# Order of the six matmuls of a weight block: by pass over both column halves, or by column half over the three passes

## The chip, the cores and the metric

One core of a Trainium2 chip runs the whole program in one launch. The metric is the device time of one execution in microseconds (us); of several runs the median is taken.

## The reference

One inference step of a two-layer decoder trunk, for a prompt of 512 tokens and 8 sample tokens that share the weights. Everything is float32.

```
x += 0.5 * SwiGLU_a(RMSNorm(x))
x += Mixer(RMSNorm(x))      # layer 0: retention and SSD heads; layer 1: latent attention
x += 0.5 * SwiGLU_b(RMSNorm(x))
...
def swiglu(h, w_in, w_out):
    gate, up = jnp.split(h @ w_in, 2, axis=-1)
    return (jax.nn.silu(gate) * up) @ w_out
```

The model width is 1024, the hidden width of the four FFNs 2816. Most of the work is these dense products: h @ w_in and the product with w_out of the FFNs, and the input and output projections of the two mixers.

## The kernel before

The 520 tokens lie along the free axis, features on the 128 partitions. A dense product is made of weight blocks of 128x128. Float32 accuracy comes from two parts of each operand in float32r: weights as `w_high` (WH) + `w_low` (WL), activations as `x_high` (XH) + `x_low` (XL), or `hidden_high` (HH) + `hidden_low` (HL) in the second product of an FFN. A block is multiplied three times ("passes"): high weights with high activations, high weights with low activations, low weights with high activations. The 520 columns are cut into two halves of 260, and each half of an output tile has an accumulator bank of its own in PSUM. So a block is six matmuls of 260 columns, each with its own weight load.

Weights come in chunks of four blocks (256 KB), issued by SP into four slots (`w_raw`). ScalarE makes the high part (line 330), VectorE the low part (line 336), and TensorE waits for the low part once per chunk (semaphore w_split). The function `gemm` (line 358 is its matmul) goes through the blocks of a step: k (128 rows of the contraction) outside, m (one or two output tiles) inside, so up to four banks are in use; the other four belong to the next step. One semaphore tells when the last matmul of a step is done (acc_full), and only then are the banks read; another tells when a chunk's weights were used (w_used). TensorE's order is written out by hand; the FFN's first product runs in a hardware loop of two steps of 16 blocks, ten times round.

Two places in the latent attention do not use `gemm`. `wo_first` (line 2443) makes the first step of the output projection, the 16 blocks of `("wo", 0)`, and it goes through all blocks for half 0 and then through all of them again for half 1:

```
for half in range(2):
    ...
    for k in range(KD):
        ...
        for m in range(2):
            ...
            for w, x, start, stop in ((wh, XH, ...), (wh, XL, ...), (wl, XH, ...)):
                mm = nc.tensor.matmul(PS[:, b0 + 2 * m + half, 0:TH], w, x[:, k, cols], ...)
```

The steps ("wo", 1) to ("wo", 3) that follow use `gemm` with the same operands XH, XL, WH and WL. The step ("uv", g) (line 2341) makes three passes of 512 columns into one bank, then three into the next.

Of the kernel before, what the change touches and what calls it, by code (L numbers as in the profile page):

```python
# [200 lines left out]
def program(nc, io, phases=PHASES):  # L201
# [66 lines left out]
    def bank0(step):  # L268
        return 4 * plan.set_of[step]
# [19 lines left out]
    def acquire(pe, step, i=None):  # L289

        n = plan.turn_of[step]
        if n:
            pe.wait_ge(acc_free[plan.set_of[step]], n if i is None else n + i)
# [45 lines left out]
    def gemm(pe, step, mtiles, ktiles, rhs, i=None, split=0, before_k=None, cols=TH):  # L339


        acquire(pe, step, i)
        first, b0 = plan.first[step], bank0(step)
        blocks = [(k, m) for k in range(ktiles) for m in range(mtiles)]
        for c in range((len(blocks) + 3) // 4):
            n = first + c
            slot = n % R
            for j, (k, m) in enumerate(blocks[4 * c:4 * c + 4]):
                if before_k and m == 0:
                    before_k(k)  # L350
                if j == 0:
                    pe.wait_ge(w_split, n + 1 if i is None else split * i + (n + 1))
                wh, wl = (w[:, slot, j * P:(j + 1) * P] for w in (WH, WL))
                xh, xl = rhs(k)
                for w, x, start, stop in ((wh, xh, k == 0, False), (wh, xl, False, False),
                                          (wl, xh, False, k == ktiles - 1)):
                    for half in range(2):
                        mm = nc.tensor.matmul(PS[:, b0 + 2 * m + half, 0:cols], w,  # L358
                                              x[:, half * cols:(half + 1) * cols], start=start, stop=stop)
            if 4 * c + 4 >= len(blocks):  # L360
                mm.then_inc(acc_full[plan.set_of[step]], 1)
            else:
                mm.then_inc(w_used, 1)
# [47 lines left out]
    e.XH, e.XH_OFF, e.XL, e.acc, e.acc_free = XH, XH_OFF, XL, acc, acc_free  # L411
    e.acc_full, e.acquire, e.at, e.bank0, e.first_wait = acc_full, acquire, at, bank0, first_wait
    e.gemm, e.halves, e.io, e.nc, e.nn_of = gemm, halves, io, nc, nn_of
    e.out_stored, e.pe_stats, e.phases, e.plan, e.sem = out_stored, pe_stats, phases, plan, sem
    e.w_split, e.w_used, e.wait_free, e.wait_full, e.x_rhs = w_split, w_used, wait_free, wait_full, x_rhs
# [50 lines left out]
    def _(pe):  # L466
        def ffn(f):
            nn = nn_of[f]
            gemm(pe, (f, "in", 0), 2, KD, x_rhs, before_k=first_wait(pe, nn))
            pe_stats(pe, (f, "in", 0), nn)  # L470
            gemm(pe, (f, "in", 1), 2, KD, x_rhs, before_k=spread_at(pe, 3, (f, "in", 0), nn))
            with pe.Fori(0, (KF - 2) // 2) as i:
                for g in (2, 3):
                    gemm(pe, (f, "in", g), 2, KD, x_rhs, i, 8)
            done = KF * (ffn_index[f] + 1)
            h_rhs = lambda k: (HH[:, k, :], HL[:, k, :])
            for g in (0, 1):

                gemm(pe, (f, "out", g), 2, KF, h_rhs,
                     before_k=(lambda k: pe.wait_ge(hl_done, done - KF + k + 1)) if g == 0 else None)  # L480
            for g in (2, 3):
                gemm(pe, (f, "out", g), 2, KF, h_rhs)
# [2429 lines left out]
```

## Time and profile before

| | |
|---|---|
| runs | 2303.39, 2304.45, 2306.28 us; median 2304.45 us |
| span of the profiled execution, first to last instruction | 2300.2 us |
| left around the span, against the median of the runs | 4.25 us |
| TensorE busy, weight loads busy | 98%, 95% of the span |
| VectorE, ScalarE, GpSimd busy | 49%, 35%, 7% |
| mean granted TensorE clock | 0.995 of full speed |

No time of its own is given for the profiled execution, so it is put at its span and the 4.25 us around it, which is the median. Busy times are sums over one engine. A matmul's row lasts longer than its share of the engine, since matmuls overlap; how fast they follow each other is read from their start times. The chain of waits names, for each moment, the instruction that the end of the program hung on.

### The profile page before, as it was taken

The page shows a single profiled execution, that of the slowest core. Times are in us where ns is not written, and L with a number is a line of the kernel's source. Part 1 is how long each engine was busy: PE and PEld are TensorE (multiplying, and loading weights), DVE is VectorE, ACT ScalarE, POOL GpSimd, SP SyncE. Part 2 cuts the span into 40 slices and gives each one's busy share as a digit, 9 for nine tenths or more (in the row PEclk, how much of TensorE's full clock was granted, in tenths as well). Part 3 has the DMA queues.
Part 4 walks back from the last instruction along what each step waited for, and adds up shares of the span by engine and source line. Part 5 has one row for each costly group of instructions (what it writes and reads, how often), then busy time and mean ns, then how long its engine had stood idle before and what let it go on. Part 6 is the DMA issues. An engine that isn't in the chain of part 4 may idle for free.

```text
span 2300.2 us, 48657 instructions
## 1 busy us (share of the span) xinstructions
PE 2258.0 (98%) x19482; PEld 2179.2 (95%) x19482; DVE 1117.0 (49%) x1773; ACT 812.2 (35%) x1420; POOL 170.9 (7%) x243
## 2 busy tenths in 40 slices
PE   9999999999999999999999999999999989999998
PEld 9999999998888999999999999999996689999997
DVE  4444434787436544444334444433557745444433
ACT  4333333462324333333233333233346634333222
POOL 0000001022100010000010000001114411000000
PEclk9999999999999999999999999999999999999999
DMA  4323333233333232333332333333546733323333
GB/s 146 91 91 91 96 101 113 79 98 101 119 118 111 84 100 84 94 92 91 102 102 88 93 92 91 99 102 91 162 151 229 264 99 92 91 91 91 96 102 106
DMA packets 119872, 249.49 MB, mean 108 GB/s; under 512 B 15360, under 2 KB 15632, under 8 KB 118400
## 3 DMA queue, kind: packets, MB, share of 16 engines
q1 hardware_dynamic: 105552, 193.05, 28.1%
q0 software_dynamic: 14048, 54.49, 6.9%
q8 instruction: 99, 1.62, 0.3%
q14 instruction: 29, 0.24, 0.0%
q10 hardware_dynamic: 144, 0.09, 0.0%
HBM read 237.30 MB, written 9.95 MB: 107 GB/s over the span
## 4 chain that ended last, share of the span: by engine, by line
PE 91%; DVE 6%; ACT 2%; issue 1%; DMA 0%; SPq 0%; DVEq 0%; ACTq 0%
PE psum L358 83%; PE psum L2356 1%; PE psum L2371 1%; DVE w_low L336 1%; PE psum L1163 1%; DVE conv_sum L1593 1%; PE psum L2443 1%; DVE probs_by_key L2783 0%; PE psum L2341 0%; PE psum L2401 0%; PE psum L1150 0%; ACT probs L2516 0%; PE psum L2323 0%; PE psum L1008 0%; PE psum L2297 0%
## 5 line engine op out<-in xcount | busy, mean ns | idle before, releaser
L336 DVE TENSOR_TENSOR w_low<-w_raw,w_high 128x512 fp32r<-128x512 f32 x718 | 510.4, 729 | 631.5 <-ACT w_high L330 630.7
L358 PE MATMUL psum<-x_high,w_high 128*128 128x260 f32 x3840 | 773.6, 283 | 5.9 <-DVE w_low L336 2.8
L358 PE MATMUL psum<-x_low,w_high 128*128 128x260 f32 x3840 | 770.5, 282 | 0.0
L358 PE MATMUL psum<-x_high,w_low 128*128 128x260 f32 x3840 | 769.3, 282 | 0.0
L358 PEld LDWEIGHTS psum<-x_high,w_high 128*128 128x128 f32 x3840 | 589.2, 188 | 12.3 <-DVE x_low L640 1.9
L330 ACT ACTIVATE w_high<-w_raw 128x512 fp32r<-128x512 f32 x718 | 433.9, 623 | 463.4 <-PE psum L358 451.6
L358 PEld LDWEIGHTS psum<-x_low,w_high 128*128 128x128 f32 x3840 | 591.8, 189 | 0.0
L358 PEld LDWEIGHTS psum<-x_high,w_low 128*128 128x128 f32 x3840 | 591.0, 188 | 0.0
L358 PE MATMUL psum<-hidden_high,w_low 128*128 128x260 f32 x1408 | 284.0, 283 | 0.0
L358 PE MATMUL psum<-hidden_high,w_high 128*128 128x260 f32 x1408 | 282.9, 282 | 0.0
L358 PE MATMUL psum<-hidden_low,w_high 128*128 128x260 f32 x1408 | 282.9, 282 | 0.0
L663 DVE TENSOR_TENSOR gate_up<-psum,rstd 128x520 f32<-128x520 f32 x176 | 114.9, 695 | 320.7 <-PE psum L358 306.4
L546 ACT ACTIVATE silu_gate<-gate_up 128x520 f32<-128x520 f32 x88 | 56.2, 639 | 528.8 <-DVE gate_up L663 528.5
L358 PEld LDWEIGHTS psum<-hidden_high,w_high 128*128 128x128 f32 x1408 | 217.4, 188 | 0.0
L358 PEld LDWEIGHTS psum<-hidden_high,w_low 128*128 128x128 f32 x1408 | 216.8, 188 | 0.0
L358 PEld LDWEIGHTS psum<-hidden_low,w_high 128*128 128x128 f32 x1408 | 216.7, 188 | 0.0
L553 ACT ACTIVATE hidden_high<-hidden 128x520 f32 (+1 forms) x88 | 56.3, 640 | 126.6 <-DVE hidden L670 126.6
L776 POOL TENSOR_TENSOR square_sums<-squares 128x520 f32<-128x520 f32 x6 | 7.9, 1320 | 1234.9 <-ACT squares L525 1234.9
L2836 POOL DMA_DIRECT2D cache_pages<-in_cache_pages_dram x128 | 68.7, 537 | 129.7 <-issue 124.7
L681 DVE TENSOR_TENSOR hidden_low<-hidden,hidden_high 128x520 f32 (+1 forms) x88 | 61.1, 694 | 3.1 <-ACT hidden_high L553 3.1
L670 DVE TENSOR_TENSOR hidden<-silu_gate,gate_up 128x520 f32<-128x520 f32 x88 | 61.1, 695 | 2.8 <-ACT silu_gate L546 2.8
L525 ACT ACTIVATE squares<-residual 128x1040 f32<-128x1040 f32 x23 | 24.7, 1075 | 91.6 <-DVE residual L695 91.6
(395 smaller groups left out, 1652.5 us busy)
## 6 DMA issues: line engine op xcount, KB each, us to landing
w_raw<-in_weights_dram SPq DMA_DIRECT2D x720, 256.0 KB, 2.7
cache_pages<-in_cache_pages_dram POOLq DMA_DIRECT2D x128, 272.0 KB, 4.3
ret_sample_state<-in_state_ret_dram POOLq DMA_DIRECT2D x2, 2048.0 KB, 8.5
out_ret_s_dram<-ret_sample_state POOLq DMA_DIRECT2D x2, 2048.0 KB, 6.6
out_y_dram<-residual SPq DMA_DIRECT2D x8, 260.0 KB, 2.2
ssm_sample_state<-in_state_ssm_dram POOLq DMA_DIRECT2D x2, 1024.0 KB, 5.6
out_ssm_s_dram<-ssm_sample_state POOLq DMA_DIRECT2D x2, 1024.0 KB, 4.7
residual<-in_x_dram SPq DMA_DIRECT2D x3, 520.0 KB, 6.7
```

Of the source, the lines that this page charges most:

```text
L330: nc.scalar.activation(WH[:, slot, :], WRAW[:, slot, :], ACT.Copy).then_inc(w_high, 1)
L336: nc.vector.tensor_tensor(WL[:, slot, :], WRAW[:, slot, :], WH[:, slot, :].bitcast(F32), ALU.subtract).then_inc(w_split, 1)
L358: mm = nc.tensor.matmul(PS[:, b0 + 2 * m + half, 0:cols], w, x[:, half * cols:(half + 1) * cols], start=start, stop=stop)
L525: nc.scalar.activation(SQT[:], XT[:, 2 * pair:2 * pair + 2, :], ACT.Square).then_inc(squares_done, 1)
L546: nc.scalar.activation(SGT[:, g % 2, :], GU[:, g % 2, 0, :], ACT.Silu).then_inc(silu_done, 1)
L553: nc.scalar.activation(out, src, ACT.Copy).then_inc(hh_done, 1)
L663: ins = nc.vector.tensor_tensor(out[:, 2 * m:2 * m + 2, :], acc(step)[:, 2 * m:2 * m + 2, :], halves(RSTD[:]), ALU.mult)
L670: nc.vector.tensor_tensor(HT[:, g % 2, :], SGT[:, g % 2, :], GU[:, g % 2, 1, :], ALU.mult).then_inc(hid_done, 1)
L681: nc.vector.tensor_tensor(out, src, hi.bitcast(F32), ALU.subtract).then_inc(hl_done, 1)
L1163: nc.tensor.matmul(PS[:, b + m, jt * P:NP_], VTOK[:, jt, m * P:(m + 1) * P], ST[:, soff[jt]:soff[jt] + n], start=jt == 0, stop=jt == NTT - 1)
L1593: ins = nc.vector.scalar_tensor_tensor(CACC[:, m, 0:NP_], cr[:, k:k + NP_], w[k], CACC[:, m, 0:NP_], ALU.mult, ALU.add)
L2836: pool.dma_start(BLOBS[c % 3][:, j, p, :], io["cache_pages"][bass.ds(idx, 1)] .rearrange("a p n -> (a p) n")).then_inc(page_loaded[c % 3], 16)
```

## The change

The loop over the halves goes outside the loop over the passes:

```diff
-                for w, x, start, stop in ((wh, xh, k == 0, False), (wh, xl, False, False),
-                                          (wl, xh, False, k == ktiles - 1)):
-                    for half in range(2):
+                for half in range(2):
+                    for w, x, start, stop in ((wh, xh, k == 0, False), (wh, xl, False, False),
+                                              (wl, xh, False, k == ktiles - 1)):
                         mm = nc.tensor.matmul(PS[:, b0 + 2 * m + half, 0:cols], w,
                                               x[:, half * cols:(half + 1) * cols], start=start, stop=stop)
```

The instructions are the same in number and operands; `wo_first` and ("uv", g) are not touched. On TensorE, at the start of a step of the FFN's first product, inside the loop, two blocks and their wait stood so before (x_high and x_low are the activations, w_high and w_low the weights; "x2" are the two halves, which go to two banks):

```order
L352 ISA [waits acc_free0]
L358 MATMUL psum<-x_high_50,w_high_53 128x260 [waits w_split_done]
L358 MATMUL psum<-x_high_50,w_high_53 128x260
L358 MATMUL psum<-x_low_51,w_high_53 128x260 x2
L358 MATMUL psum<-x_high_50,w_low_54 128x260 x2
L358 MATMUL psum<-x_high_50,w_high_53 128x260 x2
L358 MATMUL psum<-x_low_51,w_high_53 128x260 x2
L358 MATMUL psum<-x_high_50,w_low_54 128x260 x2
```

At the same place after the change:

```order
L352 ISA [waits acc_free0]
L358 MATMUL psum<-x_high_50,w_high_53 128x260 [waits w_split_done]
L358 MATMUL psum<-x_low_51,w_high_53 128x260
L358 MATMUL psum<-x_high_50,w_low_54 128x260
L358 MATMUL psum<-x_high_50,w_high_53 128x260
L358 MATMUL psum<-x_low_51,w_high_53 128x260
L358 MATMUL psum<-x_high_50,w_low_54 128x260
L358 MATMUL psum<-x_high_50,w_high_53 128x260
L358 MATMUL psum<-x_low_51,w_high_53 128x260
```

The waits stand before the same matmul as before, the first of a chunk or of a k. Within a block, banks A B A B A B became A A A B B B, and the loaded weights high high high high low low became high high low high high low. The orders of VectorE, ScalarE, GpSimd and SP are the same in both kernels.

## Rows read from the trace of the kernel before

**Rows 1.** The page: busy times of TensorE, its granted clock by slices, and the chain.

```profile
PE 2258.0 (98%) x19482; PEld 2179.2 (95%) x19482; DVE 1117.0 (49%) x1773; ACT 812.2 (35%) x1420; POOL 170.9 (7%) x243
...
PEclk9999999999999999999999999999999999999999
...
PE 91%; DVE 6%; ACT 2%; issue 1%; DMA 0%; SPq 0%; DVEq 0%; ACTq 0%
```

**Rows 2.** The page's groups of line 358: count, busy us, mean ns, idle before.

```profile
L358 PE MATMUL psum<-x_high,w_high 128*128 128x260 f32 x3840 | 773.6, 283 | 5.9 <-DVE w_low L336 2.8
...
L358 PEld LDWEIGHTS psum<-x_high,w_high 128*128 128x128 f32 x3840 | 589.2, 188 | 12.3 <-DVE x_low L640 1.9
...
L358 PEld LDWEIGHTS psum<-x_low,w_high 128*128 128x128 f32 x3840 | 591.8, 189 | 0.0
L358 PEld LDWEIGHTS psum<-x_high,w_low 128*128 128x128 f32 x3840 | 591.0, 188 | 0.0
L358 PE MATMUL psum<-hidden_high,w_low 128*128 128x260 f32 x1408 | 284.0, 283 | 0.0
```

**Rows 3.** Groups by line, TensorE: the smaller operands of line 358.

```profile
L358 PE MATMUL psum<-q_latent_high,w_high 128*128 128x260 f32 x128 | 25.9, 284 | 0.0
...
L358 PE MATMUL psum<-ssm_out_high,w_low 128*128 128x260 f32 x128 | 25.7, 282 | 0.0
...
L358 PE MATMUL psum<-kv_latent_high,w_high 128*128 128x256 f32 x32 | 6.5, 284 | 0.0
```

**Rows 4.** Waits, whole span: who waited for whom, us in total, times, longest us.

```profile
ACT w_high L330 <- PE psum L358: 451.6, 226, 3.5
...
DVE gate_up L663 <- PE psum L358: 306.4, 84, 3.9
```

**Rows 5.** Timeline, TensorE, one FFN step in the loop: start us, us, what.

```profile
1006.29 0.40 PE L358 MATMUL psum<-x_high,w_high 128*128 128x260 f32 x2
...
1007.69 0.40 PE L358 MATMUL psum<-x_high,w_high 128*128 128x260 f32 x2
...
1017.72 0.40 PE L358 MATMUL psum<-x_high,w_high 128*128 128x260 f32 x2
```

**Rows 6.** Timeline, TensorE, an FFN's second product: starts of steps 1 and 3.

```profile
1129.36 0.41 PE L358 MATMUL psum<-hidden_high,w_high 128*128 128x260 f32 x2
...
1192.68 0.41 PE L358 MATMUL psum<-hidden_high,w_high 128*128 128x260 f32 x2
```

**Rows 7.** Timeline, TensorE, wo_first: matmuls 1, 2, 13, 49 and 96.

```profile
1861.37 0.39 PE L2443 MATMUL psum<-x_high,w_high 128*128 128x260 f32 x1
1861.60 0.28 PE L2443 MATMUL psum<-x_low,w_high 128*128 128x260 f32 x1
...
1862.92 0.28 PE L2443 MATMUL psum<-x_high,w_high 128*128 128x260 f32 x1
...
1867.26 0.28 PE L2443 MATMUL psum<-x_high,w_high 128*128 128x260 f32 x1
...
1872.87 0.28 PE L2443 MATMUL psum<-x_high,w_low 128*128 128x260 f32 x1
```

**Rows 8.** Timeline, TensorE: ("wo", 1) and its block 3, ("wo", 2), the FFN behind.

```profile
1872.98 0.40 PE L358 MATMUL psum<-x_high,w_high 128*128 128x260 f32 x2
...
1874.42 0.40 PE L358 MATMUL psum<-x_high,w_high 128*128 128x260 f32 x2
...
1884.45 0.40 PE L358 MATMUL psum<-x_high,w_high 128*128 128x260 f32 x2
...
1907.30 0.40 PE L358 MATMUL psum<-x_high,w_high 128*128 128x260 f32 x2
```

**Rows 9.** Timeline, TensorE, line 2341: first and last of 48 matmuls.

```profile
1708.02 0.39 PE L2341 MATMUL psum<-w_high,kv_latent_high 128*128 128x512 f32 x1
...
1718.92 0.39 PE L2341 MATMUL psum<-w_high,kv_latent_low 128*128 128x512 f32 x1
```

## Prediction, written before the changed kernel was run

> **What bounds the kernel now.** I read the page first. TensorE is busy 98% of the span, 91% of the chain that ended last is TensorE's, and the granted clock is full in every slice [rows 1]: the program is a row of matmuls. Next come the groups of the line that the change touches. Line 358 has three forms of 3840 matmuls with x, three of 1408 with hidden, and three each of 128, 128 and 32 for the smaller operands [rows 2, 3]: 11,520 + 4,224 + 384 + 384 + 96 = 16,608 matmuls. Before the 3840 in the costliest form TensorE idles 5.9 us in all [rows 2], so nothing but the matmuls themselves sets their rate. The engines that feed and empty TensorE wait for it, not the other way round: ScalarE's weight split 451.6 us, VectorE's gate_up 306.4 us [rows 4].
>
> A row's 283 ns is not what a matmul costs, since they overlap; the spacing of starts is. One FFN step in the loop is 96 matmuls from 1006.29 to 1017.72 us: 11.43 / 96 = 119.1 ns [rows 5]. Two steps of an FFN's second product are 528 matmuls from 1129.36 to 1192.68: 119.9 ns [rows 6]. At some 119.4 ns the 16,608 matmuls take 1,983 us, 86% of the span. So the whole question is one number: by how much the new order changes that spacing. Each 0.1 ns is 1.7 us. What a measurement of this kernel can tell from no change is about 0.2%, 4.6 us, that is 0.28 ns per matmul.
>
> **The change part by part.**
>
> *Count, waits, other engines.* Nothing is added or removed: still one weight load per matmul, the same operands, the same number of columns. Each wait stays before the same first matmul of a chunk or a k, and the signals stay on the last matmul of a chunk and of a step, which is half 1 in its third pass in both orders. Readers of the banks wait for that one signal, so the first bank being finished earlier lets nobody start earlier. Chunk by chunk the weights are released at the same matmul, so SP, ScalarE and VectorE see the same times. Cost 0, and no cover is needed for it: no transfer moves.
>
> *Weight loads.* Before, four of a block's five neighbouring pairs of loads bring the same weights twice; now two do. If a repeated load were cheap, losing two repeats would cost. The rows say it isn't: in the form with x_low both loads repeat the one ahead and take 189 ns; in the two others one of two does, and they take 188 [rows 2]. Cost 0.
>
> *Three matmuls in a row into one bank.* The trace already holds this order, and it is the row that I lean on. wo_first makes three passes into one bank, then three into another, with the same operands and 260 columns as gemm's x forms. Its first gap is a stall at the start (1861.37 to 1861.60); behind it 47 gaps from matmul 2 to matmul 49 take 1861.60 to 1867.26, 120.4 ns, and the 48 from there to the first matmul of the next step, 1867.26 to 1872.98, 119.2 ns [rows 7, 8]. The three steps behind it, in the old order and with the same arrays, take 1872.98 to 1907.30 for 288 matmuls: 119.2 ns [rows 8]. So the price of the new order lies between 0 (second half of wo_first) and +1.2 ns (first half), +0.6 ns over the whole, (1872.98 - 1861.60) / 95 = 119.8. Times 16,608 the ends are 0 and +20 us, and +10 us for the whole. I take the second half, 0: it is the nearest row, directly ahead of the old order on the same data, while during the first half TensorE still picks up waits for late activations and had just stalled. A second row agrees: line 2341 puts three passes of 512 columns into a bank, 47 gaps in 10.90 us, 231.9 ns or 0.453 ns per column, against 119.2 / 260 = 0.458 in the alternating order [rows 9, 8]. A fixed toll for staying on a bank would show there.
>
> *The opening of a step.* The spacing isn't constant. In the loop the first 12 matmuls of a step (both blocks of k = 0) take 1006.29 to 1007.69, 116.7 ns; the other 84 take 10.03 us, 119.4 [rows 5]. So the spacing depends on which operands follow which. The step right behind wo_first does not have that quick opening: 1872.98 to 1874.42, 120.0 ns [rows 8], and neither has wo_first: 1861.60 to 1862.92 is 11 gaps of 120.0 [rows 7]. The only rows in the new order open slowly, so I charge the loss of the quick opening: 2.7 ns x 12 for each of 80 steps in the loops (four FFNs, ten rounds, two steps) is +2.6 us. Below, the bound is 0 (kept); a gain is not excluded, since what makes it quick isn't visible (rival 2).
>
> *Sum.* 0 + 0 + 0 + 2.6 = +2.6 us on the profiled execution, taken as its span 2300.2 and 4.25 around it, that is the median, 2304.45. Forecast: **2307 us**, +0.1%, within what can be told from no change.
>
> A rule weighs against even the small charge. The Trainium skill (TensorE: Matmul & The Clock Gate, Step-by-step: what each phase is for) says that loading the next weights takes no SBUF read bandwidth from the running matmul. By it the spacing would not depend on which load runs beside which matmul, and the sum would be 0, 2304.45 us. The rows speak against it as a full account: the same 260 columns go at 116.7, 119.1 and 119.9 ns depending on the place [rows 5, 6].
>
> **Rivals.**
>
> *1. Slower: the new order runs at wo_first's mean.* Staying on one bank, or changing weights more often, costs what all of wo_first shows, +0.6 ns. Place: every block of line 358. For it: 119.8 against 119.2 on the same arrays [rows 7, 8]. Against it: the second half shows none. Time: 16,608 x 0.6 = +10, 2314 us; it decides from 0.28 ns on. With the first half's +1.2 ns it would be 2324. A rule stands beside it. The Trainium skill (Perfetto Trace Analysis, Matmul Optimizations) asks to use all eight PSUM banks for the most parallelism. By that rule the old alternation is the better order and the kernel gets slower; line 2341 doesn't bear a toll out [rows 9], so I give it no more than this rival's chance.
>
> *2. Faster: the quick opening spreads.* If what slows k = 1 and later is a collision between the streams read for a matmul and for the next load, another order may avoid it. Ceiling: all matmuls at 116.7 instead of 119.4 is 16,608 x 2.7 = -45 us; a quarter of that is -11, 2293 us. For it: 116.7 occurs at all, in the same code. Against it: hidden at 119.9 and wo_first show no sign of it [rows 6, 7].
>
> *3. The change doesn't do what it says.* The tool chain could load weights once for like neighbours. The counts speak against it: 3840 loads for 3840 matmuls in each form [rows 2]. I give it nothing.
>
> **How the numbers follow.** No measurable change (2307, own range 2300 to 2309): 0.47. Rival 1 and milder forms of it beyond +4.6 us: 0.40, because the only rows in the new order average slower. Rival 2 and milder forms: 0.13. For 8 in 10, I take in rival 1 to somewhat past its mean price, 2318, leaving the first half's +20 us out (0.09), and rival 2's milder forms to 2299 (0.09 left below).
>
> **What would show it.** Right: in the profile after, the starts of an FFN step in the loop lie about 11.46 us apart (11.43 and 12 x 2.7 ns); its first 12 gaps now near 119 to 120 ns; two steps of the second product still 63.3 us; VectorE, ScalarE and SP rows unchanged but for the shift. Rival 1 would show as steps of 11.5 us and more (0.6 ns x 96 = 0.06 on top of 11.46) and 63.6 us for the two steps of the second product; rival 2 as steps below 11.40. A new idle time in front of line 358 would mean that my account of the waits is wrong.

## The result, and the profile after

The changed kernel takes 2310.16 us (median), the kernel before, run beside it, 2302.89. One run of the changed kernel took 5385.77 us; the others give a ratio of 1.0028, 95% interval 1.0019 to 1.0038. That is slower by 0.28%, just outside the 0.2% that I had called no change, and inside the range.

The page of the changed kernel, answering to [rows 1] and [rows 2]:

```profile
PE 2265.3 (98%) x19482; PEld 2185.1 (95%) x19482; DVE 1116.6 (48%) x1773; ACT 812.1 (35%) x1420; POOL 171.0 (7%) x243
...
PEclk9999999999999999999999999999999999999999
...
PE 91%; DVE 6%; ACT 2%; issue 1%; DMA 0%; SPq 0%; DVEq 0%; ACTq 0%
...
L358 PE MATMUL psum<-x_high,w_high 128*128 128x260 f32 x3840 | 1086.9, 283 | 6.2 <-DVE w_low L336 2.4
```

The chain, the counts and a matmul's mean of 283 ns stand as before, and so, nearly, does the idle time ahead of the group (6.2 us, before 5.9). Only the group's busy sum looks different, 1086.9 us against 773.6: two matmuls of the same group no longer follow each other, so their overlap is no longer counted once. The other engines wait for the same thing about as long as before, with [rows 4] beside it:

```profile
ACT w_high L330 <- PE psum L358: 451.2, 226, 3.5
...
DVE gate_up L663 <- PE psum L358: 311.2, 84, 3.9
```

What differs is the spacing of the matmuls. The timeline of TensorE, at the places of [rows 5] (start of the step, of k = 1 and of the next step) and of [rows 6] (second product, starts of steps 1 and 3):

```profile
1007.78 0.28 PE L358 MATMUL psum<-x_high,w_high 128*128 128x260 f32 x1
...
1009.21 0.28 PE L358 MATMUL psum<-x_high,w_high 128*128 128x260 f32 x1
...
1019.27 0.28 PE L358 MATMUL psum<-x_high,w_high 128*128 128x260 f32 x1
...
1131.23 0.28 PE L358 MATMUL psum<-hidden_high,w_high 128*128 128x260 f32 x1
...
1194.32 0.28 PE L358 MATMUL psum<-hidden_high,w_high 128*128 128x260 f32 x1
```

The step takes 11.49 us, 119.7 ns a matmul (before 11.43, 119.1); its first 12 matmuls take 1.43 us, 119.2 ns (before 116.7), the other 84 take 10.06 us, 119.8 (before 119.4). The 528 matmuls of the second product go the other way: 63.09 us, 119.5 ns, against 63.32 and 119.9.

Where the 7.4 us of span (2300.2 to 2307.6) lie follows from the starts of the stages in both timelines:

| stretch | before, us | after, us | difference |
|---|---|---|---|
| first products of the four FFNs | 255.45 + 252.68 + 252.70 + 252.69 | 257.20 + 253.89 + 253.91 + 253.89 | +5.4 |
| second products (the last one with the end of the program) | 126.64 + 126.64 + 126.63 + 140.21 | 126.20 + 126.20 + 126.20 + 139.46 | -2.1 |
| layer 0's mixer; layer 1's, up to the last small projections; ("wo", 1) to ("wo", 3) | 455.90 + 92.90 + 34.32 | 455.60 + 92.88 + 34.46 | -0.2 |
| latent attention with wo_first | 176.41 | 180.94 | +4.5 |
| start of the first matmul | 7.03 | 6.78 | -0.2 |

So the order of the six matmuls is worth about +3 us in this pair of profiles. The +4.5 us stand, but for some 0.05 us, in code that the change doesn't touch (only the 96 matmuls with kv_latent belong to `gemm`: 11.45 us before, 11.50 after), and come from the clock. Busy times and granted clock in stretches of the latent attention, of the kernel before:

```profile
1820.00:1866.00 46.00, 38.98 (x536) 29.10 (x535) 28.78 (x73) 21.33 (x58) 12.87 (x24) 1.00 0.50 170
1866.00:1872.00 6.00, 6.00 (x52) 6.00 (x52) 1.38 (x2) 1.26 (x2) 0.00 (x0) 1.00 0.10 9
```

and of the changed kernel (the columns are stretch, length, then busy time and count on TensorE, its weight loads, VectorE, ScalarE and GpSimd, then the granted clock, the DMA share and GB/s):

```profile
1820.00:1866.00 46.00, 38.06 (x489) 26.74 (x489) 30.30 (x75) 23.18 (x67) 13.40 (x25) 0.93 0.53 180
1866.00:1872.00 6.00, 6.00 (x56) 5.98 (x54) 0.45 (x2) 0.26 (x1) 0.00 (x0) 0.72 0.01 3
```

The clock is 0.93 and 0.72 where it was 1.00. In the first of the two stretches TensorE is busy 38.98 of 46 us before and 38.06 after. wo_first shows the low clock matmul by matmul:

```profile
1866.66 0.53 PE L2443 MATMUL psum<-x_high,w_high 128*128 128x260 f32 x1
1866.99 0.42 PE L2443 MATMUL psum<-x_low,w_high 128*128 128x260 f32 x1
...
1869.80 0.42 PE L2443 MATMUL psum<-x_high,w_low 128*128 128x260 f32 x1
...
1870.33 0.28 PE L2443 MATMUL psum<-x_high,w_low 128*128 128x260 f32 x1
...
1879.80 0.28 PE L358 MATMUL psum<-x_high,w_high 128*128 128x260 f32 x1
```

From 1866.99 to 1869.80 there are 13 gaps of 216 ns, the lower of the two levels (1.2 GHz), and matmuls of 0.42 us; then 0.28 us again. wo_first takes 13.14 us against 11.61. This stretch is not the new order's alone: over the fourteen profiles of this study the latent attention takes 176.2 to 176.5 us in five (the kernel before and e2 in the old order, e1, e7 and e9 in the new), and 178.2 to 181.0 in nine, seven of which have the old order with x. How often it comes can be read from the granted clock of each run, averaged over the run: this is 0.995 or 0.996 in the five profiles with the short latent attention, and 0.994 or less in the nine with the long one. By that mark the low clock came in 33 of 99 runs of the kernel before, and in 21 of 27 runs of the new order in the same layout (all 7 of the changed kernel, 7 of 10 each of e1 and e11, described below). It also costs more there: the span of the kernel before averages 2300.0 us without it and 2303.6 with it, that of e1 and e11 2302.2 and 2308.0. So of the measured +0.28% some 2 to 3 us are spacing, and the rest is a low clock that comes more often with the new order. Why it does is open.

### The profile page after: what moved, and what is told of

Same layout as the page of the kernel before. It is cut to its first block, busy times and chain, and to the rows that moved or that the text cites. A ratio compares the mean times of both kernels' runs of the same rounds, so it can differ in the third digit from the quotient of the medians.

```text
span 2307.6 us, 48657 instructions
## 1 busy us (share of the span) xinstructions
PE 2265.3 (98%) x19482; PEld 2185.1 (95%) x19482; DVE 1116.6 (48%) x1773; ACT 812.1 (35%) x1420; POOL 171.0 (7%) x243
## 4 chain that ended last, share of the span: by engine, by line
PE 91%; DVE 6%; ACT 2%; issue 1%; DMA 0%; SPq 0%; DVEq 0%; ACTq 0%
PE psum L358 83%; PE psum L2356 1%; PE psum L2371 1%; DVE w_low L336 1%; PE psum L1163 1%; DVE conv_sum L1593 1%; PE psum L2443 1%; DVE probs_by_key L2783 0%; PE psum L2341 0%; PE psum L2401 0%; PE psum L2323 0%; ACT probs L2516 0%; PE psum L1150 0%; PE psum L1008 0%; PE psum L2297 0%
## 5 line engine op out<-in xcount | busy, mean ns | idle before, releaser
L358 PE MATMUL psum<-x_high,w_high 128*128 128x260 f32 x3840 | 1086.9, 283 | 6.2 <-DVE w_low L336 2.4
L358 PE MATMUL psum<-x_low,w_high 128*128 128x260 f32 x3840 | 1085.0, 283 | 0.0
L358 PE MATMUL psum<-x_high,w_low 128*128 128x260 f32 x3840 | 1083.6, 282 | 0.0
L358 PEld LDWEIGHTS psum<-x_high,w_high 128*128 128x128 f32 x3840 | 723.3, 188 | 13.2 <-issue 2.3
L358 PEld LDWEIGHTS psum<-x_low,w_high 128*128 128x128 f32 x3840 | 723.0, 188 | 0.1
L358 PEld LDWEIGHTS psum<-x_high,w_low 128*128 128x128 f32 x3840 | 723.1, 188 | 0.0
L330 ACT ACTIVATE w_high<-w_raw 128x512 fp32r<-128x512 f32 x718 | 433.8, 623 | 468.0 <-PE psum L358 451.2
L358 PE MATMUL psum<-hidden_high,w_low 128*128 128x260 f32 x1408 | 397.3, 282 | 0.0
L358 PE MATMUL psum<-hidden_low,w_high 128*128 128x260 f32 x1408 | 397.1, 282 | 0.0
L358 PE MATMUL psum<-hidden_high,w_high 128*128 128x260 f32 x1408 | 396.3, 281 | 0.0
L663 DVE TENSOR_TENSOR gate_up<-psum,rstd 128x520 f32<-128x520 f32 x176 | 114.9, 694 | 325.4 <-PE psum L358 311.2
L358 PEld LDWEIGHTS psum<-hidden_high,w_low 128*128 128x128 f32 x1408 | 265.1, 188 | 0.0
```

The source lines that it names most:

```text
L330: nc.scalar.activation(WH[:, slot, :], WRAW[:, slot, :], ACT.Copy).then_inc(w_high, 1)
L358: mm = nc.tensor.matmul(PS[:, b0 + 2 * m + half, 0:cols], w, x[:, half * cols:(half + 1) * cols], start=start, stop=stop)
L663: ins = nc.vector.tensor_tensor(out[:, 2 * m:2 * m + 2, :], acc(step)[:, 2 * m:2 * m + 2, :], halves(RSTD[:]), ALU.mult)
```

## Experiments

The theories at the start: B, staying on one bank costs; W, the more frequent change of weights costs; O, the sequence of operands costs, whatever the bank; A, a form of O in which the addresses of operands decide. All kernels are compared with the kernel before, run on the same chip. "x" is the mean spacing in the loop steps of the FFNs' first products, "hidden" that in their second products (ns), both from the starts in the trace.

| run | order of the six | ratio (95% interval) | x | hidden |
|---|---|---|---|---|
| before | old | 1 | 119.03 | 119.92 |
| after | new | 1.0028 (1.0019 to 1.0038) | 119.65 | 119.50 |
| e1_alternate_banks | new, old sequence of banks | 1.0021 (1.0011 to 1.0032) | 119.65 | 119.50 |
| e2_stay_on_bank | old, new sequence of banks | 0.9998 (0.9989 to 1.0007) | 119.03 | 119.92 |
| e11_snake | new, passes of half 1 reversed | 1.0023 (1.0012 to 1.0033) | 119.65 | 119.51 |
| e4_hidden_only | new with hidden alone | 0.9991 (0.9981 to 1.0001) | 119.03 | 119.50 |
| e3_weights_first | old, arrays moved by multiples of 512 B | 1.0000 (0.9990 to 1.0010) | 119.03 | 119.92 |
| e5_weights_32 | old, weights 32 B higher | 0.9995 (0.9985 to 1.0005) | 119.02 | 119.92 |
| e6_weights_follow | old, weights follow the k tiles | 1.0039 (1.0026 to 1.0053) | 120.07 | 118.9 or 120.1 |
| e7_follow_new_order | new, layout of e6 | 1.0036 (1.0024 to 1.0049) | 119.5 or 119.8 | 118.9 or 120.6 |
| e8_aligned | old, high and low weights side by side | 1.0033 (1.0023 to 1.0044) | 120.07 | 119.5 or 120.1 |
| e9_aligned_new_order | new, layout of e8 | 1.0035 (1.0022 to 1.0049) | 119.5 or 119.8 | 119.5 to 120.6 |
| e10_entry | old, e8 with k = 0 entered from 32 B below | 0.9974 (0.9964 to 0.9984) | 117.0 or 120.2 | 117.0 to 120.2 |
| e12_sweep | old, e8 with a climb over three k | 1.0029 (1.0019 to 1.0039) | 119.79 | 119.80 |

**The bank.** Two kernels separate the sequence of operands from that of banks. The first has the new sequence of operands and goes to the banks in turns:

```diff
+                passes = ((wh, xh), (wh, xl), (wl, xh))
+                for p, (half, (w, x)) in enumerate((half, wx) for half in range(2) for wx in passes):
+                    mm = nc.tensor.matmul(PS[:, b0 + 2 * m + p % 2, 0:cols], w, x[:, half * cols:(half + 1) * cols],
+                                          start=k == 0 and p < 2, stop=k == ktiles - 1 and p >= 4)
```

> The order of operands and weight loads of the change (half 0 with its three passes, then half 1), but the six matmuls of a block write their two banks in turn, A B A B A B, as before the change. So the sums of the two halves land in mixed banks. Theory O (which operands are read next to which sets the spacing, the bank does not): FFN steps in the loop stay 11.49 us apart and two steps of the second product 63.1 us, as after the change; 1.003 of the kernel before. Theory B (staying on one bank for three matmuls costs): back to 11.43 and 63.3 us; 1.000.

The second keeps the old sequence of operands and stays three matmuls on a bank:

```diff
+                for p, (half, (w, x)) in enumerate((half, wx) for wx in passes for half in range(2)):
+                    mm = nc.tensor.matmul(PS[:, b0 + 2 * m + p // 3, 0:cols], w, x[:, half * cols:(half + 1) * cols],
+                                          start=k == 0 and p % 3 == 0, stop=k == ktiles - 1 and p % 3 == 2)
```

> The mirror image: the order of operands and loads of the kernel before (each pass over both halves), but the six matmuls of a block write A A A B B B. The sums of the two halves land in mixed banks. Theory O: FFN steps stay 11.43 us apart with the quick opening of 12 matmuls at 116.7 ns, second product 63.3 us; 1.000. Theory B: 11.49 us and more; 1.003.

The timelines, first of the alternating banks (start of a step, of k = 1, of the next step):

```profile
1007.84 0.28 PE L357 MATMUL psum<-x_high,w_high 128*128 128x260 f32 x1
...
1009.27 0.28 PE L357 MATMUL psum<-x_high,w_high 128*128 128x260 f32 x1
...
1019.33 0.28 PE L357 MATMUL psum<-x_high,w_high 128*128 128x260 f32 x1
```

then of the old sequence that stays on a bank:

```profile
1006.21 0.40 PE L357 MATMUL psum<-x_high,w_high 128*128 128x260 f32 x2
...
1007.61 0.40 PE L357 MATMUL psum<-x_high,w_high 128*128 128x260 f32 x2
...
1017.63 0.40 PE L357 MATMUL psum<-x_high,w_high 128*128 128x260 f32 x2
```

1.43 and 11.49 us are the numbers of the changed kernel, 1.40 and 11.42 to 0.01 us those of the kernel before. The bank costs nothing; B falls. The first of the two also had its latent attention at full clock (176.2 us) and a span of 2303.2 us: +3.0 over the 2300.2 of before, the same +3 us that the table by stretches leaves to the order.

**The number of weight changes.** Of a block's five neighbouring pairs of matmuls, one changes the weights in the old order and three do in the new. With half 1's passes run backwards two do:

```diff
+                for half in range(2):
+                    for p, (w, x) in enumerate(passes[::-1] if half else passes):
```

> Halves outside as in the change, in the layout of before, but half 1 takes its passes backwards: weights high high low | low high high. So a block changes its weights as often as before the change (twice with the step to the next block) and not four times, while each bank still takes three matmuls in a row. Theory W (each change of weights costs): the spacing of before, 119.0 in the loop and 119.9 ns in the second product, 1.000. Theory A (it is the distances of the operands that run beside each other, in their sequence): a third set of spacings, neither that of before nor that of the change, between 118.5 and 120.5 ns; the 96 spacings of a step match neither; 0.996 to 1.007.

TensorE's timeline (second and third matmuls of the step's first block, third of k = 1's, second of the next step):

```profile
1008.99 0.28 PE L358 MATMUL psum<-x_low,w_high 128*128 128x260 f32 x1
1009.11 0.41 PE L358 MATMUL psum<-x_high,w_low 128*128 128x260 f32 x2
...
1010.54 0.28 PE L358 MATMUL psum<-x_high,w_low 128*128 128x260 f32 x1
...
1020.48 0.28 PE L358 MATMUL psum<-x_low,w_high 128*128 128x260 f32 x1
```

The step is 11.49 us and k = 0 is 1.43: the changed kernel again, and so are all 96 spacings, where W asks for something between the two. W falls. The third set of spacings that an account by addresses had been given here did not come either; but w_high and w_low lie 8192 B apart, so an account that goes by the low bits of addresses, as the one below, asks for none. What the changed kernel and this one have in common, and the old order has not, is the sequence of the activations: the column halves go 0 0 0 1 1 1 against 0 1 0 1 0 1, and the parts high low high high low high against high high low low high high. Which of the two counts is not separated by any run.

**Only the second product.** The new order where it had been faster:

```diff
+                order = [(half, p) for half in range(2) for p in passes] if ktiles == KF else \
+                    [(half, p) for p in passes for half in range(2)]
```

> The changed order in the FFN's second product alone (22 k tiles); all other steps in the order of before. Theory O: second product 63.1 us for two steps against 63.3, which over 4,224 matmuls at -0.42 ns is -1.8 us, and steps in the loop 11.43 us as before; 0.9992. Theory B: the second product no faster, 1.000 or above.

```profile
1128.84 0.28 PE L359 MATMUL psum<-hidden_high,w_high 128*128 128x260 f32 x1
...
1191.93 0.28 PE L359 MATMUL psum<-hidden_high,w_high 128*128 128x260 f32 x1
```

63.09 us, as in the changed kernel, with x at its old 119.03 ns. The effects of the two products are separate. The ratio 0.9991 agrees with 4,224 x 0.42 ns = -1.8 us, but its interval ends at 1.0001.

**Addresses.** The halves of a k tile begin 1040 B apart (260 x 4), the k tiles 2080 B, weight blocks 512 B. First the weight arrays were put below x_high and x_low; every distance changes by a multiple of 512 B:

```diff
-    XH, XH_OFF = sb("x_high", [P, KD, T], F32R)
-    XL, XL_OFF = sb("x_low", [P, KD, T], F32R)
...
+    XH, XH_OFF = sb("x_high", [P, KD, T], F32R)
+    XL, XL_OFF = sb("x_low", [P, KD, T], F32R)
```

> The kernel before with nothing changed but the place of five arrays in SBUF: the weight slots (w_raw, w_high, w_low) lie below x_high and x_low instead of above them. Order, banks and operands are those of before. Theory A (a closer form of O: addresses that the matmul and the load beside it read set the spacing): the spacing in the loop moves by 0.2 ns or more from 119.1, either way, and the quick opening of a step changes; 0.995 to 1.005. Theory B, and a theory that only the order of loads counts: 11.43 us per step, 119.9 ns in the second product, to the nanosecond as before; 1.000.

Nothing moved: 119.03 and 119.92, and the theory's own number missed. What can still matter is the distance's low part. So the weights, and with them all that lies above them, hidden too, were moved up by 32 B against x:

```diff
     XL, XL_OFF = sb("x_low", [P, KD, T], F32R)
+    cursor[0] += 32
```

> The kernel before, with the weight slots (and all that lies above them) 32 bytes higher in SBUF; x_high and x_low stay where they are. In the run with the weights laid below x all distances between the two had changed by a multiple of 512 bytes only, and the spacing was the same to the nanosecond. Theory A (the distance of the matmul's operand from the weights being loaded, in its low bits, sets the spacing): the quick opening of a step (116.7 ns, at k = 0 where x and weights lie a multiple of 256 bytes apart) is lost or moves, and the 96 spacings of a step become others; FFN steps 11.43 us +- 0.03 or more. Theory S (the sequence alone, or where x itself lies): 11.43 us, the same 96 spacings, quick opening kept.

The starts of k = 0, 1 and 2 and of the next step:

```profile
1004.01 0.40 PE L359 MATMUL psum<-x_high,w_high 128*128 128x260 f32 x2
...
1005.43 0.40 PE L359 MATMUL psum<-x_high,w_high 128*128 128x260 f32 x2
...
1006.83 0.40 PE L359 MATMUL psum<-x_high,w_high 128*128 128x260 f32 x2
...
1015.43 0.40 PE L359 MATMUL psum<-x_high,w_high 128*128 128x260 f32 x2
```

Now k = 0 takes 1.42 us and k = 1 takes 1.40, 116.7 ns a matmul: the quick opening has moved by one k. Means of 12 spacings for k = 0 to 7, before: 116.8, 119.0, 119.6, 120.2, 119.4, 119.5, 119.1, 118.6; with the shift: 118.5, 116.8, 119.0, 119.6, 120.2, 119.4, 119.5, 119.1. It is the same row, turned by one place. A k tile lies 2080 = 8 x 256 + 32 B behind the one ahead of it, so k = 1 now has the distance, up to multiples of 256 B, that k = 0 had, and k = 0 that of k = 7. Hidden moved along with the weights, and its 119.92 stayed. The row of spacings goes with the low bits of the distance from weights to activations.

**One distance for all k.** If the distance alone decided, then weights that are padded by 32 B per k, so that all k have the distance of k = 0, should all run at 116.7 ns. (They have it in the first and the last FFN. The two between begin in the third of the four weight slots, chunks 254 and 390 against 0 and 580, and with the padding that slot lies 128 B further on, modulo 256 B: all k have one distance there too, but another.)

```diff
-    WH, WH_OFF = sb("w_high", [P, R, CW], F32R)
-    WL, _ = sb("w_low", [P, R, CW], F32R)
+    WH, WH_OFF = sb("w_high", [P, R, 2, CW // 2 + 8], F32R)
+    WL, _ = sb("w_low", [P, R, 2, CW // 2 + 8], F32R)
```

> The order of before, but the weight blocks in w_high and w_low are padded by 32 bytes per k, as x tiles are 2080 = 4 x 512 + 32 bytes apart; so in steps of 8 k tiles every k has the distance between x and weights that k = 0 has (the base of all arrays lies 128 bytes lower to make room, and two small tables move). Theory A: the quick pace of the opening holds over the whole step, 96 x 116.7 = 11.20 us in place of 11.43; over some 11,000 matmuls that is -25 us, 0.989; the second product, whose distances change too, may go either way by 0.5 ns, 2 us. Theory S: 11.43 us, 1.000.

```profile
1007.73 0.40 PE L360 MATMUL psum<-x_high,w_high 128*128 128x260 f32 x2
...
1009.17 0.40 PE L360 MATMUL psum<-x_high,w_high 128*128 128x260 f32 x2
...
1019.25 0.40 PE L360 MATMUL psum<-x_high,w_high 128*128 128x260 f32 x2
```

All k became alike, as the theory had it, but at the wrong value: 11.52 us, 120.07 ns, with the same 12 spacings eight times (122, 117, 116, 122, 124, 123, 120, 120, 117, 119, 122, 119). These lines are of the second FFN; the first and the last, at the distance of k = 0 itself, have other spacings (118, 124, 118 and 120 in turn for the most part) and the same mean of 120.07. The kernel is slower, 1.0039. The same layout with the new order, by the diff of the change itself:

> The same padded weights with the changed order of matmuls. Theory A: every k goes as k = 0 does in the changed kernel, 12 matmuls in about 1.43 us, so steps of 11.42 us in place of 11.49 and 2 per cent or so behind the old order in this layout. Theory S: 11.49 us as in the changed kernel, 1.003.

Also slower, 1.0036. Here w_low lay at another distance than w_high, modulo 512 B. Next both parts lay side by side, and hidden was moved to the distance of x:

```diff
+    W2, WH_OFF = sb("w_high_low", [P, R, 2, 2 * CW // 2 + 8], F32R)
+    WH, WL = W2[:, :, :, 0:CW // 2], W2[:, :, :, CW // 2:CW]
...
+    HH = at("hidden_high", [P, KF, T], REGION + 128, F32R)
+    HL = at("hidden_low", [P, KF, T], REGION + 192 + KF * T * 4, F32R)
```

> The order of before. High and low weights of two blocks now lie side by side (1024 + 1024 bytes) with 32 bytes behind them, so that for every k of a step of 8 k tiles x_high lies at a multiple of 512 bytes from w_high and w_low, and x_low 256 bytes off that, as at k = 0 before; hidden_high and hidden_low are put at the same distances for the first 8 of their 22 k tiles (then 256 bytes off, then again the same). Theory A with the period of 512 bytes that the runs so far leave: the opening pace, 116.7 ns, holds over whole steps, 96 x 116.7 = 11.20 us in place of 11.43, 27 us over 11,520 matmuls; the second product goes from 119.9 to between 116.7 and 118.5 ns, 63.3 to 61.6 us or a little more for two steps, 6 to 14 us: 0.982 to 0.986 of the kernel before. If it is not the distance to both parts of the weights, the steps stay at 11.4 us or above and the ratio at 0.998 to 1.005.

And again with the diff of the change on top:

> The same layout with the changed order of matmuls. Theory A: every k goes as k = 0 goes in the changed kernel, 12 matmuls in 1.43 us, 11.45 us a step, so the change then costs 2 per cent of a step: 1.000 to 1.003 against the kernel before, 1.017 or so against the aligned kernel in the old order. If the order did not matter by itself, it would be as quick as that one, 0.985.

Neither is quick: 120.07 ns with x in the old order, with the twelve spacings of e6, and in ten of sixteen steps of the second products as well, where the distance goes on by 256 B behind k = 7. So the period is 256 B at most, and the constant distance isn't what made k = 0 quick. What k = 0 had besides, in the kernel before, was other distances behind it.

**The way in.** The layout of e8, with the blocks of k = 0 in every eight 32 B higher (those that lie first in slot 0), so that a constant distance is entered from another one (`first` is where a slot's weights begin, in elements of 4 B, `step` lies between its two k):

```diff
-    WH, WL = W2[:, :, :, 0:CW // 2], W2[:, :, :, CW // 2:CW]
+        for s in range(R):
+            first, step = (8, CW) if s == 0 else (2 * s * (CW + 8), CW + 8)
+            pair = W2[:, first:first + 2 * step].rearrange("p (h n) -> p h n", h=2)
```

> The aligned layout in the order of before, with one difference: the weight block of slot 0 that holds k = 0 (in the second product k = 0, 8 and 16) lies 32 bytes higher, so x comes from 32 bytes below the common distance there and at the common distance from k = 1 on. In the kernel before and in the one with all weights 32 bytes higher, each quick opening (116.7 ns) stood where the distance goes to a multiple of 256 bytes from 32 below it; in the aligned kernel, where it stays there from the start, all k went at 120.1 ns. Theory H (the spacing has a memory: which of several steady patterns holds at a distance depends on how it was entered): from k = 1 on the steps run at 116.7 ns, k = 0 at 118 to 121: 11.20 to 11.25 us a step, -22 us over the steps with x, the second product near 117 ns, -12 us: 0.983 to 0.990. Rival N (no memory; the quick opening needs something else, such as the wait at the start of a step): 120.1 ns at all k but the first, 11.5 us, 1.003.

This one beats both kernels, 2297.35 us, 0.9974 (0.9964 to 0.9984), but stays far from theory H's 0.983 to 0.990. Its loops do not run alike. TensorE in 160 us each of the four first products, with the count of matmuls and the granted clock:

```profile
80.00:240.00 160.00, 160.00 (x1370) 1.00 0.30 92
880.00:1040.00 160.00, 160.00 (x1334) 1.00 0.31 92
1250.00:1410.00 160.00, 160.00 (x1333) 1.00 0.31 92
1930.00:2090.00 160.00, 160.00 (x1370) 1.00 0.31 91
```

1370 and 1334 matmuls in the same time, at the same clock, with the same instructions in the loop. Two steps from its timeline, the rows with x_low of the first block of a step and of the next, first in the first FFN, then in the second:

```profile
101.12 0.40 PE L371 MATMUL psum<-x_low,w_high_low 128*128 128x260 f32 x2
...
112.36 0.40 PE L371 MATMUL psum<-x_low,w_high_low 128*128 128x260 f32 x2
...
1003.32 0.40 PE L371 MATMUL psum<-x_low,w_high_low 128*128 128x260 f32 x2
...
1014.86 0.40 PE L371 MATMUL psum<-x_low,w_high_low 128*128 128x260 f32 x2
```

11.24 us against 11.54: 117.0 and 120.2 ns a matmul. From the third step on, each FFN's first product holds one pattern to its end. But the addresses are not the same: in the two FFNs between, which begin in the third slot, the distance is 128 B another and the shifted blocks are those of k = 4. The traces show it: k = 4 stands out in the second FFN (121.0 ns, the other k at 120.0 to 120.2), k = 0 in the first (118.9, the other k at 116.8). So 117.0 against 120.2 is a difference of layout, and theory H was put to the test in the first and the last FFN alone.

There it holds: k = 1 to 7 run at 116.8 ns where e8, at the same distances, has 120.07. The two differ in k = 0 alone, so the spacing depends on what ran before, up to seven k back. The second product of the first FFN shows it at equal addresses. Its four steps use the same slots and the same hidden; TensorE in 29 us of each, with the count of matmuls and the granted clock:

```profile
259.00:288.00 29.00, 29.00 (x250) 1.00 0.36 101
290.00:319.00 29.00, 29.00 (x245) 1.00 0.35 102
321.50:350.50 29.00, 29.00 (x250) 1.00 0.36 102
352.50:381.50 29.00, 29.00 (x245) 1.00 0.34 101
```

The first and third step run at 117.0 ns, the second and fourth at 119.5. The set of banks alternates from step to step as well, but it does so in the loops too, where the steps are all alike; and in e8 the first step runs at 120.07 and the third, with the same banks, at 119.52. So the same sequence of distances has more than one steady pattern.

**A longer way in.** The kernel before climbs through several distances ahead of its quick k = 0. The last run copies that, with the first three k of eight 96, 64 and 32 B higher:

```diff
-            first, step = (8, CW) if s == 0 else (2 * s * (CW + 8), CW + 8)
+            first, step = ((24, CW), (1048, CW), (2080, CW + 8), (3120, CW + 8))[s]
```

> Old order of the six matmuls. As in the run before it, high and low weights lie side by side and k tiles 2080 B apart as the activations do, but the weights of the first three k tiles of every eight lie 96, 64 and 32 B higher, so that the distance from weights to activations climbs to its steady value in four steps of 32 B, as it does ahead of the quick opening in the kernel before. Theory H (the spacing depends on the distances of the matmuls just behind as well, and such a climb leads into the quick pattern): three k at about 119.5 ns and five at 116.7 to 117.0, that is 117.8 ns, 11.31 us for a step of an FFN's first product against 11.43, two steps of the second product near 62.2 us against 63.3; 20 to 23 us off, a ratio of 0.990 to 0.991. Rival M (which pattern holds is decided by more than the last three k tiles): a mixture of steps at 117 and at 120 ns, with the same code and the same layout, as in the run before it; ratio 0.996 to 1.003. Rival Z (the pattern reached by the climb lasts one k only, and then goes back to the slow one): 119.5 to 120 ns in all steps, ratio 1.000 to 1.004.

```profile
1010.21 0.41 PE L371 MATMUL psum<-x_low,w_high_low 128*128 128x260 f32 x2
...
1021.71 0.41 PE L371 MATMUL psum<-x_low,w_high_low 128*128 128x260 f32 x2
```

11.50 us a step, 119.79 ns in every loop, and 1.0029: the numbers of the rival without a lasting quick pattern, and a miss for the theory's. (These lines are of the second FFN, where the climb stands at k = 4 to 6; in the first it stands at k = 0 to 2.) No k of either is quick: in the first FFN they run at 119.3 to 120.8 ns. The climb does not lead into the quick pattern. Which history does is open, and so is which two reads meet.

## Why the prediction was right or wrong

**What bounds the kernel, and the waits: right.** 98% busy, the same chain, the waits of ScalarE for line 358 at 451.2 us (451.6 before) and of VectorE at 311.2 (306.4). No wait and no transfer took part. That one number, the spacing, decides what the change itself does was right too.

**Bank and weight loads at 0: right,** and now shown by themselves: the bank by e1 and e2, the weight changes by e11. So the mechanism of rival 1 is wrong. The Trainium skill (Perfetto Trace Analysis, Matmul Optimizations) asks for all eight banks to be used for parallelism. Both orders use all eight, so I read too much into it when I took it for a word on the sequence within a block; and there 11.42 us a step is the same with three matmuls in a row on a bank as in turns.

**The price of the order: the step that failed.** I took wo_first's second half, 119.2 ns, for the new order with x, and put its 119.8 over the whole down to late activations. So I charged 0 for it. Measured is +0.62 ns in the loop steps: the new order runs at 119.65, and the three ("wo") steps behind wo_first, which it equalled in its second half, now take 34.46 us for 288 matmuls, 119.65 too. The mean of the whole of wo_first, rival 1's +0.6 ns, came nearer, but that it is the same cost is not shown: wo_first stays on one column half for 48 matmuls, the change for three. And rival 1 had tied it to a mechanism that falls, and multiplied it by all 16,608. Hidden was a second mistake in the same step: I gave it x's price, with no row of its own, and it gained 0.42 ns. Layer 0's mixer, with x as well, starts most of its steps behind waits; its -0.3 us says little, since over the fourteen profiles it takes 453.8 to 457.3 us. The sum, +5.4 - 2.1 - 0.2 - 0.2, is +3 us, near the +2.6 forecast, but by luck: a term too small and a term left out cancel.

**The quick opening: right in sign, and only a part.** It went, as charged: 116.7 to 119.2 ns, 12 x 2.5 = 0.03 us a step. The other 0.03 us of a step's 0.06 come from the 84 matmuls behind it (119.4 to 119.8), charged at 0. Rival 2, the faster kernel, came true for hidden alone, and without its quick spacing: 119.5 ns, not 116.7.

**What the sum did not hold:** the latent attention, +4.5 us in this pair of profiles, by the clock. I had taken the granted clock as given, and it falls more often with the new order (21 of 27 runs against 33 of 99). With it the changed kernel is outside 0.2%, so no measurable change, the case to which I gave the most weight, did not come; with spacing alone (+3 us, 0.13%) it would have.

**The rule on weight loads.** The traces show that 32 B more between weights and activations turn the row of spacings by one k, with no instruction changed. The Trainium skill (TensorE: Matmul & The Clock Gate, Step-by-step: what each phase is for) has the load of the next weights take no read bandwidth from the running matmul. By that the weights' place should not matter, and here it does, between 116.7 and 120.2 ns; that the loads are what collides is not shown.

## What to carry to other kernels

Where TensorE is 98% busy and nothing waits, look at the spacing of starts, k by k: differences of half a nanosecond in the mean repeat from step to step, and a regrouping of the same matmuls moves them. When a row seems to show the new arrangement, check that it has the same sequence of operands, don't take the half of it that suits, and look for a row of its own for each operand. Where weights go round in slots, work out in which slot each stage begins before calling two loops alike. Before a layout is built on such a number, run one kernel for each suspect (bank, weight changes, addresses): here the two that seemed likely cost nothing.

## What the hardware showed that I had not expected

The time between matmuls of 260 columns depends on the distance from weights to activations modulo 256 B (e5, e8), on the sequence of the activations (e1, e2 and e11), and on what ran before: in e10 steps with the same instructions and addresses run at 117.0 and 119.5 ns, at a granted clock of 1.00. The quick pattern everywhere would be worth 16,608 x 2.4 ns = 40 us against the kernel before (an estimate, from 119.4 and 117.0); none of these layouts holds it throughout.

The latent attention falls to the lower level of the clock in some executions and not in others, with either order: 176.2 us with the new order (e1), 180.8 with the old one with x (e4). With the new order it does so more often, though nearly all the code of this stretch is the same.
